# The first stage of a two-block transformer kernel: modulation by columns, token roots in the identity, squares by 16 transfers

## The reference, cut to what matters

```python
h_res = x.astype(jnp.float32)              # 1 x 2048 x 1024
c_act = jax.nn.silu(c.astype(jnp.float32)) # 1 x 1024
mod = c_act @ w_ada[l] + b_ada[l]          # 1024 x 3072
shift, scale, gate = jnp.split(mod, 3, axis=-1)
h = rmsnorm(h_res, norm_w[l]) * (1.0 + scale[:, None, :]) + shift[:, None, :]
y = hybrid_mixer(h, ...)
# rmsnorm(x, w) = x * lax.rsqrt(mean(x * x, axis=-1) + EPS) * w
```

## Time and profile before

| | us |
|---|---|
| median of 3 runs | 3389.2 |
| lowest and highest | 3387.11, 3394.51 |
| profiled execution | 3392.7 |
| its span, first to last instruction | 3390.9 |
| TensorE busy in the span | 3304.6 (97%) |

### The profile page before, as it was taken

How to read it: one execution, slowest core, us unless ns; L and a number is a source line. 1 busy time by engine, 2 the same in 40 slices (tenths; PEclk the granted TensorE clock), 3 DMA queues, 4 the chain that set the end, 5 groups by cost and what they waited for, 6 DMA issues and landing times. The chain is left out here.

```text
span 3390.9 us, 43856 instructions
## 1 busy us (share of the span) xinstructions
PE 3304.6 (97%) x16379; PEld 1809.4 (53%) x16379; DVE 1298.2 (38%) x2804; ACT 1020.3 (30%) x2409; POOL 922.7 (27%) x705
## 2 busy tenths in 40 slices
PE   8999999998999999899999999999999999899999
PEld 4485858584455454444445544554455455445544
DVE  3333434346244243444224332442243234545522
ACT  4314141413234143233124423442343234311100
POOL 1002020204542533633321125113411431161232
PEclk8999999999999999999999999999999999999999
DMA  6111010103120212332111132113211321240321
GB/s 227 30 30 38 21 38 13 33 17 99 47 48 16 50 29 87 107 109 84 52 35 39 45 87 78 39 51 88 71 39 54 92 64 39 63 114 13 143 93 62
DMA packets 229949, 210.82 MB, mean 62 GB/s; under 512 B 69404, under 2 KB 194732, under 8 KB 225600
## 3 DMA queue, kind: packets, MB, share of 16 engines
q1 hardware_dynamic: 226636, 208.01, 20.8%
q10 hardware_dynamic: 3104, 0.01, 0.1%
HBM read 157.98 MB, written 50.01 MB: 61 GB/s over the span
## 5 line engine op out<-in xcount | busy, mean ns | idle before, releaser
L608 PE MATMUL m<-hT,roll 128*128 128x512 f32 x704 | 321.1, 593 | 1.3 <-ACT pre L758 1.3
L2479 PE MATMUL d<-hT,roll 128*128 128x512 f32 x648 | 296.2, 600 | 2.3 <-PEq L76 2.3
L2479 PE MATMUL joint<-hT,roll 128*128 128x512 f32 x624 | 284.4, 598 | 0.0
L2516 POOL TENSOR_TENSOR w_z<-w_u,w_y 128x512 f32<-128x512 f32 x40 | 50.8, 1270 | 723.7 <-ACT w_y L2485 723.7
L1420 PE MATMUL n<-hT,roll 128*128 128x512 f32 x512 | 228.0, 601 | 1.8 <-PEq L76 1.8
L2479 PE MATMUL joint<-w_room,roll 128*128 128x512 f32 x488 | 220.7, 595 | 0.0
L2479 PE MATMUL d<-w_room,roll 128*128 128x512 f32 x472 | 214.2, 596 | 1.7 <-DVE w_x L2508 1.7
L2479 PEld LDWEIGHTS d<-hT,roll 128*128 128x128 f32 x648 | 122.7, 192 | 153.4 <-issue 152.8
L3176 ACT ACTIVATE mix_f<-sneg,negmax 128x192 f32<-128x192 f32 (+1 forms) x384 | 161.3, 422 | 109.2 <-DVE negmax L3328 108.5
L2479 PEld LDWEIGHTS joint<-hT,roll 128*128 128x128 f32 x624 | 115.5, 190 | 137.2 <-issue 135.9
L608 PEld LDWEIGHTS m<-hT,roll 128*128 128x128 f32 x704 | 124.9, 191 | 116.1 <-issue 115.8
(11 more groups left out here) (437 smaller groups left out, 5523.4 us busy)
## 6 DMA issues: line engine op xcount, KB each, us to landing
roll<-in_w_in SPq DMA_DIRECT2D x128, 256.0 KB, 3.1
mix_f<-alpha SPq DMA_DIRECT2D x48, 192.0 KB, 6.3
xg<-in_x SPq DMA_DIRECT2D x4, 2048.0 KB, 16.2
roll<-in_w_in SPq DMA_DIRECT2D x16, 512.0 KB, 3.9
rb<-r_rows SPq DMA_DIRECT2D x16, 512.0 KB, 4.9
mix_ml<-in_x SPq DMA_DIRECT2D x16, 512.0 KB, 3.4
x<-mix_ml SPq DMA_DIRECT2D x16, 512.0 KB, 3.0
o_rows<-mix_f SPq DMA_DIRECT2D x8, 1024.0 KB, 5.1
```

The source lines that it names most:

```text
L608: last = nc.tensor.matmul(bank[n % 2][:], w[:, k], hT[:, k, (n % 4) * TB:(n % 4 + 1) * TB], start=(k == 0), stop=(k == KC - 1))
L2479: last = nc.tensor.matmul(bank[self.bank_of(n, j, i)][:], w[:, k], x[k], start=(k == 0), stop=(k == h - 1))
L2516: nc.gpsimd.tensor_tensor(self.z[:], u, self.y[:], ALU.add).then_inc(self.pooled, 1)
```

## The change

Four things change, all of them in `modulate_and_norm`.

- `modulation(n)`: a chunk is now all 1024 rows of 256 columns, still 1 MB, in pieces of 1 KB. A block of 128 x 128 of w_ada is the weights and one column of c_act moves: 8 products sum one column of 128 results in ps_mod. Rows, their copies and the column turns (L313) go.
- Bias and norm_w come as rows (`b_rows`), 24 of 128 numbers, and one transpose behind chunk 4 turns them; VectorE copies the result to b_col.
- VectorE multiplies the identity by the reciprocal roots of a token tile (`diag`, two sets of four) in place of the rows of xg, and a turn is a product with that diagonal matrix in place of a transpose. ps_x has 7 banks instead of 4.
- x comes in 16 transfers of 512 KB, each with a semaphore; ScalarE squares all 16 tiles in that order, ahead of all reading out. VectorE reads out groups 0 and 1 and half of groups 2 and 3, ScalarE the other half.

```diff
-        ada = [roll.rows[:, 2 * i:2 * i + 2].rearrange("p s (k n) -> p (s k) n", n=TB) for i in range(NB - 1)] + [sb("ada", [P, h, TB])[:, :, :]]
+        ada = [roll.rows[:, 2 * i:2 * i + 2].rearrange("p s (k n) -> p (s k) n", n=W) for i in range(NB - 1)] + [sb("ada", [P, KC, W])[:, :, :]]
...
-        ps_x = ps("ps_x", [P, 4, TB])
+        ps_x = ps("ps_x", [P, NX, TB])
...
+        read_by_act = [(2, 2), (2, 4), (2, 6), (2, 7), (3, 0), (3, 2), (3, 4), (3, 6)]
+        read_by_dve = [(g, k) for g in range(NTB) for k in range(KC) if (g, k) not in read_by_act]
...
-                    sp.dma_start(ada[n % NB], w_v[:, h * i:h * i + h, j * TB:(j + 1) * TB]).then_inc(ada_in[n % NB], 16)
+                    sp.dma_start(ada[n % NB], w_v[:, :, n * W:(n + 1) * W]).then_inc(ada_in[n % NB], 16)
+
+                def load_rows(g):
+                    for j in range(4 * g, 4 * g + 4):
+                        sp.dma_start(xg[:, g, j % 4], x_v[:, j]).then_inc(x_in[j], 16)
...
-                sp.dma_start(xg[:, 0], x_v[:, 0]).then_inc(x_in[0], 16)
+                load_rows(0)
                 load(6)
                 load(7)
-                sp.dma_start(ident[:], t["ident"]).then_inc(ident_in, 16)
                 for g in range(1, NTB):
-                    sp.dma_start(xg[:, g], x_v[:, g]).then_inc(x_in[g], 16)
+                    load_rows(g)
...
-                square_up(0)
-                square_up(1)
+                for g in range(NTB):
+                    square_up(g)
                 act.wait_ge(gain_out, 1)
-                read_out(0)
-                square_up(2)
-                square_up(3)
-                for g in range(1, NTB):
-                    read_out(g)
+                for g, k in read_by_act:
+                    act.wait_ge(turned, KC * g + k + 1)
+                    nc.scalar.activation(hT[:, k, g * TB:(g + 1) * TB], ps_x[:, (KC * g + k) % NX], ACT.Identity, bias=mod[:, k:k + 1], scale=gain[:, k:k + 1]).then_inc(out_act, 1)
...
-                        nc.vector.tensor_scalar(xg[:, g, j % 4], xg[:, g, j % 4], rstd[:, j:j + 1], None, ALU.mult).then_inc(scaled, 1)
-
-                def row(j):
-                    dve.wait_ge(ada_used, 2 * j + 2)
-                    nc.vector.tensor_copy(mod_row[:, j * TB:(j + 1) * TB], ps_row[:, j % 2]).then_inc(row_out, 1)
+                        nc.vector.tensor_scalar(diag[:, g % 2, j % 4], ident[:], rstd[:, j:j + 1], None, ALU.mult).then_inc(scaled, 1)
...
+                for g, k in read_by_dve:
+                    dve.wait_ge(turned, KC * g + k + 1)
+                    nc.vector.tensor_scalar(hT[:, k, g * TB:(g + 1) * TB], ps_x[:, (KC * g + k) % NX], gain[:, k:k + 1], mod[:, k:k + 1], ALU.mult, ALU.add).then_inc(out_dve, 1)
+                    if (g, k) == (0, 5):
+                        scale_diagonals(1)
+                    if (g, k) == (1, 3):
+                        scale_diagonals(2)
+                    if (g, k) == (2, 1):
+                        scale_diagonals(3)
...
-                            last = nc.tensor.transpose(ps_x[:, k % 4, j * P:(j + 1) * P], xg[:, g, j, k * P:(k + 1) * P], ident[:])
+                            last = nc.tensor.matmul(ps_x[:, (KC * g + k) % NX, j * P:(j + 1) * P], xg[:, g, j, k * P:(k + 1) * P], diag[:, g % 2, j], start=True, stop=True)
...
-                def modulation(j):
-                    need(pe, row_out, j - 1)
-                    for i in range(2):
-                        n = 2 * j + i
-                        pe.wait_ge(ada_in[n % NB], 16 * (n // NB + 1))
-                        for k in range(h):
-                            last = nc.tensor.matmul(ps_row[:, j % 2], c_act[:, h * i + k:h * i + k + 1], ada[n % NB][:, k], start=(i == 0 and k == 0), stop=(i == 1 and k == h - 1))
-                        last.then_inc(ada_used, 1)
+                def modulation(n):
+                    pe.wait_ge(ada_in[n % NB], 16 * (n // NB + 1))
+                    for m in range(2):
+                        for k in range(KC):
+                            last = nc.tensor.matmul(ps_mod[:, 2 * n + m:2 * n + m + 1], ada[n % NB][:, k, m * P:(m + 1) * P], c_act[:, k:k + 1], start=(k == 0), stop=(k == KC - 1))
+                    last.then_inc(ada_used, 1)
...
-                for m in range(2 * KC):
-                    last = nc.tensor.matmul(ps_mod[:, m:m + 1], mod_row[:, m * P:(m + 1) * P], one[:], start=True, stop=True)
-                last.then_inc(mod_turned, 1)
-                pe.wait_ge(ident_in, 16)
+                for n in range(N_CHUNKS):
+                    modulation(n)
+                    if n == 4:
+                        pe.wait_ge(ident_in, 16)
+                        pe.wait_ge(smalls, 32)
+                        nc.tensor.transpose(ps_x[:, NX - 1, 0:3 * KC], b_rows[:], ident[0:3 * KC, 0:3 * KC]).then_inc(b_turned, 1)
```

More of the change, by code:

```diff
@@ L145, in modulate_and_norm @@
         NB = 5
-        h = KC // 2
-        ada = [roll.rows[:, 2 * i:2 * i + 2].rearrange("p s (k n) -> p (s k) n", n=TB) for i in range(NB - 1)] + [sb("ada", [P, h, TB])[:, :, :]]
+        NX = 7
+        W = 2 * P
+        ada = [roll.rows[:, 2 * i:2 * i + 2].rearrange("p s (k n) -> p (s k) n", n=W) for i in range(NB - 1)] + [sb("ada", [P, KC, W])[:, :, :]]
         xg = sb("xg", [P, NTB, 4, D])
         ident = sb("ident0", [P, P])
+        diag = sb("diag0", [P, 2, 4, P])
         c_col = sb("c_col", [P, KC])
-        b_col = sb("b_col", [P, 2 * KC])
-        nw = sb("nw", [P, KC])
-        one = sb("one0", [1, 1])
+        b_rows = sb("b_rows", [3 * KC, P])
+        b_col = sb("b_col", [P, 3 * KC])
         mod = sb("mod", [P, 2 * KC])
@@ L159, in modulate_and_norm @@
         rstd = sb("rstd0", [P, NT])
-        junk = hT[:, 0, T - D:T]
-        mod_row = hT[0:1, KC - 1]
+        junk = hT[:, KC - 1, T - D:T]
         ps_mod = ps("ps_mod", [P, TB])
-        ps_row = ps("ps_row", [1, 2, TB])
-        ps_x = ps("ps_x", [P, 4, TB])
+        ps_x = ps("ps_x", [P, NX, TB])
         c_in = sem("m_c_in")
@@ L168, in modulate_and_norm @@
         ada_in = [sem(f"m_ada{i}") for i in range(NB)]
-        x_in = [sem(f"m_x{i}") for i in range(NTB)]
+        x_in = [sem(f"m_x{j}") for j in range(NT)]
         ada_used = sem("m_ada_used")
         silu_c = sem("m_silu_c")
-        row_out = sem("m_row_out")
-        mod_turned = sem("m_mod_turned")
+        b_turned = sem("m_b_turned")
+        b_out = sem("m_b_out")
         mod_out = sem("m_mod_out")
@@ L183, in modulate_and_norm @@
         out_dve = sem("m_out_dve")
-        x_v = t["x"].rearrange("a (g j p) d -> p (a g) j d", p=P, j=4)
+        x_v = t["x"].rearrange("a (j p) d -> p (a j) d", p=P)
         w_v = t["w_ada"].rearrange("a (k p) n -> p (a k) n", p=P)
[L186 to L193, removed]
+        N_CHUNKS = 2 * D // W
+        read_by_act = [(2, 2), (2, 4), (2, 6), (2, 7), (3, 0), (3, 2), (3, 4), (3, 6)]
+        read_by_dve = [(g, k) for g in range(NTB) for k in range(KC) if (g, k) not in read_by_act]
         with nc.Block() as block:
@@ L198, in load @@
                 def load(n):
-                    j, i = divmod(n, 2)
                     need(sp, ada_used, n - NB + 1)
-                    sp.dma_start(ada[n % NB], w_v[:, h * i:h * i + h, j * TB:(j + 1) * TB]).then_inc(ada_in[n % NB], 16)
+                    sp.dma_start(ada[n % NB], w_v[:, :, n * W:(n + 1) * W]).then_inc(ada_in[n % NB], 16)
+                def load_rows(g):
+                    for j in range(4 * g, 4 * g + 4):
+                        sp.dma_start(xg[:, g, j % 4], x_v[:, j]).then_inc(x_in[j], 16)
                 sp.dma_start(c_col[:], t["c"].rearrange("a (k p) -> p (a k)", p=P), allow_slow_non_contiguous=True).then_inc(c_in, 16)
@@ L218, in _ @@
             def _(act):
-                nc.scalar.dma_start(b_col[:], t["b_ada"][:, 0:2 * D].rearrange("a (k p) -> p (a k)", p=P), allow_slow_non_contiguous=True).then_inc(smalls, 16)
-                nc.scalar.dma_start(nw[:], t["norm_w"].rearrange("a (k p) -> p (a k)", p=P), allow_slow_non_contiguous=True).then_inc(smalls, 16)
+                nc.scalar.dma_start(ident[:], t["ident"]).then_inc(ident_in, 16)
+                nc.scalar.dma_start(b_rows[0:2 * KC], t["b_ada"][:, 0:2 * D].rearrange("a (k p) -> (a k) p", p=P)).then_inc(smalls, 16)
+                nc.scalar.dma_start(b_rows[2 * KC:3 * KC], t["norm_w"].rearrange("a (k p) -> (a k) p", p=P)).then_inc(smalls, 16)
                 act.wait_ge(c_in, 16)
                 nc.scalar.activation(c_act[:], c_col[:], ACT.Silu).then_inc(silu_c, 1)
-                act.wait_ge(eps_out, 2)
+                act.wait_ge(eps_out, 1)
                 def square_up(g):
-                    act.wait_ge(x_in[g], 16)
                     for j in range(4 * g, 4 * g + 4):
+                        act.wait_ge(x_in[j], 16)
                         need(act, summed, j)
@@ L232, in square_up, with scale_diagonals @@
```

(43 more changed lines are left out.)

## The result

| | us |
|---|---|
| kernel before, median of 4 runs (lowest, highest) | 3388.5 (3387.1, 3394.5) |
| changed kernel, median of 4 runs (lowest, highest) | 3417.3 (3415.1, 3421.0) |
| ratio, from the single runs | 1.0082, interval 1.0066 to 1.0098 |
| forecast for the median | 3413.0 (3404 to 3424) |
| changed kernel, profiled execution and its span | 3421.0, 3419.2 |

A forecast was written before the change was run, and what follows sets the result against it. TensorE, busy 97% of the span, was taken to set the first stage's pace: modulation to 62.9, turns 31.0, end 1.6, barrier at 95.5 instead of 71.69, 23.8 us more. Median 3413.0, range 3404 to 3424.

The forecast's parts named there:

- Counting instructions: First stage on TensorE: 32 + 16 matmul calls (96 pairs) become 256 pairs; 128 transposes become 256 pairs.
- The modulation at 1.2 GHz: Modulation: 256 pairs at 0.215 us, 55.0 us, plus 0.2 for the transpose of b_rows, ending at 62.9.
- The open point, whether loads of 128 rows hold the clock: Rival in the modulation: such loads bring full clock back, modulation ends at 38.6, barrier 2.7 us faster; chance 0.15.
- When it starts: Modulation's first product: at 7.65 us, when the first chunk landed before; not under 4.7, up to 1.5 later allowed.
- The queues: SP's loads of chunks 5 to 7 issued at about 14.5, 21.4 and 28.3; x and weights landed by about 49.
- a cover: Margin of ScalarE's last four squares, ending near 54, ahead of the modulation's end at 62.9: 9 us.
- The turns: Turning x on TensorE: 21 pairs slow, 235 at 0.1125 us, together 31.0 us; reading out hidden, the 5.08 us gap gone.
- the bounds: Time until the turns regain full clock: 5.80 us the first time before, within 3.4 the second; 4.6 taken.
- The end: From the last turn to the next stage's first product: 1.61 us, kept as before.
- the sign named under what would show it: Granted clock 0.50 from the first product to some us into the turns, about 6.9 us a chunk.

The follow-up runs named there:

- run 3: Changed kernel with eight products of 512 columns of ones ahead of the modulation, one execution; the next stage's first product on TensorE at 92.63 us.
- run 7: The changed kernel again with no edit, beside the kernel before: median 3415.4 against 3391.0, ratio 1.0078.
- runs 6 and 7: The first: kernel before plus 27 products of 512 columns behind its last turn, a pure delay, median 3414.0 against 3389.9; the second has its own line.
- the last version: Changed kernel with 128 moved columns, diagonals only in groups 1 and 2, scaled rows transposed in 0 and 3: 3383.0 against 3390.4 for the kernel before, ratio 0.9978.

## Why the prediction was right

By its steps, forecast first:

- *Counting instructions*: 256 pairs in the modulation, 256 in the turns. Both counts are in the timeline.
- *The modulation at 1.2 GHz*, 55.0 + 0.2 us: 54.9 in all. The price came from L313, whose weights have one row; with 128 rows it is the same 0.215. The open point, whether loads of 128 rows hold the clock, is closed by run 3: in that stream they didn't. The Trainium skill, "TensorE: Matmul & The Clock Gate", section "LDWEIGHTS (loading the stationary operand)", prices a load by its columns over 1.2 GHz, by estimate 107 ns for 128 columns. Run 3 agrees with it at a granted clock of 1.00 (35 pairs in 3.70 us, 0.106 each) and takes twice that at 0.50 (104 in 22.00, 0.21 each).
- *When it starts*: 7.65 taken, 7.36 measured.
- *The queues*: chunks 5 to 7 expected to be issued at 14.5, 21.4 and 28.3; SP issued chunk 5 at 14.34 and chunk 6 at 21.17. The last root was ready at 51.3, where the last squares were put near 54: a cover of 11 us, not 9.
- *The turns*, 31.0 us: 30.65. They got the clock back after 3.0 us, just outside the 3.4 to 5.8 of the bounds, which by itself saved some 0.7; 0.3 of it went again in the one wait for a set of diagonals. In run 7 the turns took 31.28. A set of diagonals cost VectorE 1.1 us (1.2 estimated) and stayed hidden but for that wait.
- *The end*, 1.6: 1.68. Sum 95.5, measured 94.61.

Two things were off. The median came 4.3 us above the forecast although the barrier came 0.9 below: the forecast took every us behind the barrier as unchanged, and took one profile of before for all its executions. In three later places the two traces differ by 1.9, 0.7 and 2.9 us, and in all three the clock stood at 0.50 for longer in the trace of the changed kernel; the stage of before itself ends up to 2 us apart. The traces of runs 6 and 7, with 3318.4 and 3318.8 us behind the barrier, show that the changed kernel pays no steady cost there; why the clock fell as it did in one execution stays open. The forecast lies 2 us below the lowest of the four executions, so its range, and not its middle, held this scatter. And the sign named under what would show it, a granted clock of 0.50 in the modulation, was badly chosen: the column prints 1.00 ahead of the first recorded change, which the rows of before had shown. The pace was the sign that held.

## What to carry to other kernels

Where a matmul has few columns to move, price it by its loads and at the clock that such a stream keeps, not at the clock of the stream it replaces: holding the big operand as weights made 30 us of products into 55. If that form is wanted all the same, moving 127 idle copies of the column cost nothing here and brought the full pace back, which was worth 25 us at the barrier (94.61 against 69.46). And a factor folded into an f32 transpose turns one pair into two; do that only where TensorE would otherwise wait, as in group 2 of the last version.

## What the runs showed that I had not expected

- 128 moved columns took half the time of one (0.111 us a pair against 0.215), 32 the same time as one.
- A granted clock of 1.00 is printed for stretches ahead of the first recorded change, at half the pace: 55 us of them in the changed kernel.
- A gap of 5.42 us in TensorE cost more than itself: the 64 transposes behind it took 9.93 us, where 32 in a stream took 3.66.
